# Handing over a pair's sums bank by bank in a gated linear-recurrence block

## What is computed

```python
q, v, g = jnp.split(a @ w_in, [HG_KEY_W, HG_KEY_W + HG_VAL_W], axis=-1)
z = jnp.einsum('bld,wdk->wblk', a, w_f).astype(f32)
z = jnp.clip(z, -GATE_CLIP, GATE_CLIP)
log_f = jax.nn.log_sigmoid(z) + jnp.log1p(lb * jnp.exp(-z))
k = _heads((1.0 - lb) * jax.nn.sigmoid(-z), HG_HEADS)
q = _heads(jax.nn.silu(q.astype(f32)), HG_HEADS) * (HG_DK ** -0.5)
v = _heads(v.astype(f32), HG_HEADS)
```

## Time and profile before

| what | us |
|---|---|
| median of 3 runs | 1992.04 (1991.76 to 1995.71) |
| the profiled execution | 1992.16 |
| its span, first to last instruction | 1990.4 |
| TensorE busy | 1855.9 (93%) |
| VectorE busy | 1289.5 (65%) |
| ScalarE busy | 885.1 (44%) |

### The profile page before, as it was taken

How to read it: one execution, slowest core, us unless ns; L and a number is a source line. 1 busy time by engine, 2 the same in 40 slices (tenths; PEclk the granted TensorE clock), 3 DMA queues, 4 the chain that set the end, 5 groups by cost and what they waited for, 6 DMA issues and landing times.

```text
span 1990.4 us, 32031 instructions
## 1 busy us (share of the span) xinstructions
PE 1855.9 (93%) x13348; PEld 1699.5 (85%) x13348; DVE 1289.5 (65%) x1995; ACT 885.1 (44%) x1197; POOL 0.2 (0%) x4
## 2 busy tenths in 40 slices
PE   6668999999999999999879999999999999999998
PEld 3217888889888879898779988999999999999997
DVE  5686387878797868796995556555545555444445
ACT  5555254435353525363644445333333333344444
POOL 0000000000000000000000000000000000000000
PEclk9899999999999999999999999999999999999999
DMA  7884454444444444444466545777667676555553
GB/s 270 278 279 153 161 167 127 139 143 140 130 138 129 148 142 143 135 130 135 153 202 210 180 149 152 220 214 229 213 215 219 219 218 203 173 185 180 184 183 110
DMA packets 175378, 353.20 MB, mean 177 GB/s; under 512 B 12737, under 2 KB 80642, under 8 KB 174594
## 3 DMA queue, kind: packets, MB, share of 16 engines
q1 hardware_dynamic: 175234, 351.16, 55.1%
HBM read 346.92 MB, written 4.19 MB: 176 GB/s over the span
## 4 chain that ended last, share of the span: by engine, by line
PE 75%; DVE 17%; issue 3%; ACT 2%; DMA 2%; SPq 0%; ACTq 0%; DVEq 0%
PE bank L1048 18%; PE bank L1049 17%; PE bank L1050 17%; DVE wlo L628 4%; DVE aacc L714 3%; PE score L1151 2%; PE bank L1083 2%; PE bank L1084 2%; PE bank L1085 2%; DMA raw<-in_w_ada_dram 2%; DVE work L776 1%; PE score L1048 1%; PE score L1049 1%; PE score L1050 1%; DVE work L806 1%
## 5 line engine op out<-in xcount | busy, mean ns | idle before, releaser
L628 DVE TENSOR_TENSOR wlo<-raw,whi 128x1024 fp32r<-128x1024 f32 x520 | 636.3, 1224 | 558.0 <-ACT whi L389 557.3
L389 ACT ACTIVATE whi<-raw 128x1024 fp32r<-128x1024 f32 x520 | 551.2, 1060 | 906.2 <-PE bank L1050 654.3
L1048 PE MATMUL bank<-ahi,whi 128*128 128x256 f32 (+1 forms) x2912 | 894.9, 307 | 44.9 <-DVE wlo L628 19.6
L1049 PE MATMUL bank<-alo,whi 128*128 128x256 f32 (+1 forms) x2912 | 884.8, 304 | 0.0
L1050 PE MATMUL bank<-ahi,wlo 128*128 128x256 f32 (+1 forms) x2912 | 884.2, 304 | 0.0
L1048 PEld LDWEIGHTS bank<-ahi,whi 128*128 128x128 f32 x2912 | 561.2, 193 | 76.5 <-DVE wlo L628 23.7
L1050 PEld LDWEIGHTS bank<-ahi,wlo 128*128 128x128 f32 x2912 | 561.3, 193 | 21.4
L1049 PEld LDWEIGHTS bank<-alo,whi 128*128 128x128 f32 x2912 | 561.6, 193 | 19.0
L1083 PE MATMUL bank<-whi,ahi 128*128 128x256 f32 x512 | 150.7, 294 | 17.2 <-DVE arena L732 9.9
L714 DVE SCALAR_TENSOR_TENSOR aacc<-aw,cs,aacc 128x1024 f32<-128x1024 f32 x120 | 153.4, 1278 | 4.1 <-DMA aw<-in_w_ada_dram 3.5
L1084 PE MATMUL bank<-wlo,ahi 128*128 128x256 f32 x512 | 145.8, 285 | 0.0
(11 more groups left out here) (199 smaller groups left out, 1756.4 us busy)
## 6 DMA issues: line engine op xcount, KB each, us to landing
aw<-in_w_ada_dram SPq DMA_DIRECT2D x128, 512.0 KB, 4.8
raw<-in_ffn_w_gate_dram SPq DMA_DIRECT2D x88, 512.0 KB, 3.8
raw<-in_ffn_w_up_dram SPq DMA_DIRECT2D x88, 512.0 KB, 3.7
...
raw<-in_hg_w_in_dram SPq DMA_DIRECT2D x128, 256.0 KB, 3.0
raw<-in_hg_w_f_dram SPq DMA_DIRECT2D x128, 256.0 KB, 3.1
...
```

Of the source, the lines that this page charges most:

```text
L389: act.activation(whi[:, ck % SPL, :], raw[:, ck % RAW, :], ACT.Copy).then_inc(s_hi, 1)
L628: dve.tensor_tensor(wlo[:, ck % SPL, :], raw[:, ck % RAW, :], whi[:, ck % SPL, :].bitcast(F32), ALU.subtract).then_inc(s_lo, 1)
L1048: pe.matmul(dst, w, ah, start=start, stop=False, skip_group_check=True)
L1049: pe.matmul(dst, w, al, start=False, stop=False, skip_group_check=True)
```

## The change

Three things are done, in the VQ and Z chunks alone:

- TensorE's order within a chunk. In chunk 7, both slices of bank 0 come first, then bank 1, then bank 2, and TensorE signals `s_vd` as bank 0 and bank 1 are complete. In chunk 15 the order is bank 0, 2, 1, 3, with `s_zd` after each of the first three. Chunks 0 and 8 (`r == 0`) likewise take a bank's two slices one behind the other: chunk 8 does bank 3, then 0, 1, 2, and chunk 0 does bank 0, 2, 1. The other chunks keep their order. TensorE's part of the scan stays in the middle of the chunk.
- The values are copied by ScalarE, in place of VectorE, right behind the `hi` of chunk 8 and ahead of its scan steps, each bank as it is complete.
- VectorE clips the gates right behind the `lo` of chunk 16, ahead of scan steps and `ada`, three of the banks on their own signal, and the last on `s_used`.

The core of the diff:

```diff
@@ ScalarE
+            def values(pr):
+                if pr >= 2:
+                    act.wait_ge(s_o, 2 * pr - 2)
+                for i in range(2):
+                    act.wait_ge(s_vd, 2 * pr + i + 1)
+                    act.activation(vals[pr % 2][:, 2 * i:2 * i + 2, :], bank[i][:, :].rearrange("p (t v) -> p t v", t=2),
+                                   ACT.Copy).then_inc(s_vev, 1)
...
             for ck, kind, u, r, tasks in positions():
                 if ck > C_B + KD // 2:
                     hi(ck)
+                if kind == "Z" and r == 0:
+                    values(u)
@@ VectorE
             def clip_gates(pr):
-                dve.wait_ge(s_used, C_B + 16 * (pr + 1))
...
                 for i, (d, h) in enumerate(UNITS):
+                    if i < 3:
+                        dve.wait_ge(s_zd, 3 * pr + i + 1)
+                    else:
+                        dve.wait_ge(s_used, C_B + 16 * (pr + 1))
...
-            def values(pr):
-                dve.wait_ge(s_used, C_B + 16 * pr + 8)
...
                     lo(ck)
+                p = ck % 16
+                if p == 0 and C_B + 16 <= ck <= C_G:
+                    clip_gates((ck - C_B) // 16 - 1)
...
-                if kind == "Z" and r == 0:
-                    values(u)
-                if p == 0 and C_B + 16 <= ck <= C_G:
-                    clip_gates((ck - C_B) // 16 - 1)
@@ TensorE
+            def chunk_vq(ck, r, u, between):
+
+                if r == 0:
+                    order = ((0, 0), (1, 0), (0, 2), (1, 2), (0, 1), (1, 1))
+                elif r == 7:
+                    order = ((0, 0), (1, 0), (0, 1), (1, 1), (0, 2), (1, 2))
+                else:
+                    order = ((0, 0), (0, 2), (0, 1), (1, 0), (1, 2), (1, 1))
+                for i, (a, f) in enumerate(order):
+                    if i == 3:
+                        beside(ck, between)
...
+                    last = q_bank(ck, r, a, u) if f == 2 else v_bank(ck, r, a, u, f)
+                    if r == 7 and a == 1 and f < 2:
+                        last.then_inc(s_vd, 1)
+                last.then_inc(s_used, 1)
+
+            def chunk_z(ck, r, u, between):
+                if r == 0:
+                    order = [(a, f) for f in (3, 0, 1, 2) for a in range(2)]
+                elif r == 7:
+                    order = [(a, f) for f in (0, 2, 1, 3) for a in range(2)]
+                else:
+                    order = [(a, f) for a in range(2) for f in (3, 0, 1, 2)]
+                for i, (a, f) in enumerate(order):
+                    if i == 4:
+                        beside(ck, between)
+                    last = z_bank(ck, r, a, u, f)
+                    if r == 7 and a == 1 and f < 3:
+                        last.then_inc(s_zd, 1)
+                last.then_inc(s_used, 1)
```

More of the change, by code:

```diff
@@ L209, in build @@
         s_used = sem("chunk_used")
+        s_vd = sem("v_bank_summed")
+        s_zd = sem("z_bank_summed")
         s_aw = [sem(f"aw_in{i}") for i in range(2)]
@@ L1050, in three, with v_bank @@
                 return pe.matmul(dst, wl, ah, start=False, stop=stop, skip_group_check=True)
+            def v_bank(ck, r, a, u, half):
+                s, k = ck % SPL, 2 * r + a
+                first, end = k == 0, k == KD - 1
+                if first and u:
+                    pe.wait_ge(s_zc, 4 * (u - 1) + 1 + 2 * half)
+                o = slice(512 * a, 512 * a + 256)
+                for t in (2 * half, 2 * half + 1):
+                    dst = bank[half][:, (t % 2) * T:(t % 2 + 1) * T]
+                    tk = slice(t * P, (t + 1) * P)
+                    st = first and t % 2 == 0
+                    pe.matmul(dst, ahi[:, k, tk], whi[:, s, o], start=st, stop=False, skip_group_check=True)
+                    pe.matmul(dst, ahi[:, k, tk], wlo[:, s, o], start=False, stop=False, skip_group_check=True)
+                    last = pe.matmul(dst, alo[:, k, tk], whi[:, s, o], start=False, stop=end, skip_group_check=True)
+                return last
@@ new lines, in q_bank @@
+            def q_bank(ck, r, a, u):
+                s, k = ck % SPL, 2 * r + a
+                first, end = k == 0, k == KD - 1
+                if first and u:
+                    pe.wait_ge(s_zc, 4 * (u - 1) + 2)
+                for f in range(2):
+                    o = slice(512 * a + 256 + f * P, 512 * a + 256 + (f + 1) * P)
+                    last = three(bank[2][:, f * T:(f + 1) * T], whi[:, s, o], wlo[:, s, o],
+                                 ahi[:, k, T:TT], alo[:, k, T:TT], first and f == 0, end)
+                return last
@@ new lines, in z_bank @@
+            def z_bank(ck, r, a, u, f):
+                s, k = ck % SPL, 2 * r + a
+                first, end = k == 0, k == KD - 1
+                if first and f == 3:
+                    if u:
+                        pe.wait_ge(s_zc, 4 * u)
+                        if ada_ended(ck):
+                            pe.wait_ge(s_av, ada_ended(ck))
+                if first and f < 2:
+                    pe.wait_ge(s_vev, 2 * u + f + 1)
+                if first and f == 2:
+                    pe.wait_ge(s_qev, u + 1)
+                o = slice(512 * a + f * P, 512 * a + (f + 1) * P)
+                return three(bank[f][:, :], whi[:, s, o], wlo[:, s, o], ahi[:, k, :], alo[:, k, :], first, end)
@@ new lines, in beside @@
+            def beside(ck, between):
+                for j, n in between:
+                    scan(j, n)
+                for e in ada_ends(ck):
+                    sum_modulation(e)
+            def chunk_vq(ck, r, u, between):
[8 more added lines that the diff above has]
+                        beside(ck, between)
+                    k = 2 * r + a
+                    if u == 0:
+                        pe.wait_ge(s_al, 2 * (k + 1))
+                    last = q_bank(ck, r, a, u) if f == 2 else v_bank(ck, r, a, u, f)
+                    if r == 7 and a == 1 and f < 2:
+                        last.then_inc(s_vd, 1)
+                last.then_inc(s_used, 1)
@@ L1052, in chunk @@
             def chunk(ck, kind, r, u=0, between=()):
+                if kind == "VQ":
+                    return chunk_vq(ck, r, u, between)
+                if kind == "Z":
+                    return chunk_z(ck, r, u, between)
                 s = ck % SPL
@@ L1056, in chunk @@
                     if a:
[L1057 to L1060, removed]
+                        beside(ck, between)
                     k = 2 * r + a
                     first, end = k == 0, k == KD - 1
-                    if ck < C_B + 8 and kind == "VQ":
-                        pe.wait_ge(s_al, 2 * (k + 1))
                     if kind == "FF" and u == 0:
@@ L1066, in chunk @@
                         pe.wait_ge(s_al, 2 * KD + k + 1)
[L1067 to L1107, removed]
@@ new lines, in chunk @@
+                    tk = slice(T, TT) if kind == "G" else slice(0, T)
+                    bb = 2 * (u % 2)
+                    for f in range(4):
+                        if kind == "G" and u == 0 and first and f % 2 == 0:
+                            pe.wait_ge(s_zc, 4 * (PAIRS - 1) + 1 + f)
+                        o = slice(512 * a + f * P, 512 * a + (f + 1) * P)
+                        last = three(bank[bb + f // 2][:, (f % 2) * T:(f % 2 + 1) * T], whi[:, s, o], wlo[:, s, o],
+                                     ahi[:, k, tk], alo[:, k, tk], first and f % 2 == 0, end)
```

6 lines of the change are left out of this document (removed).

## The result

| | us |
|---|---|
| before, median of 5 runs | 1993.47 (1991.76 to 1995.71) |
| after, median of 5 runs | 1983.41 (1980.55 to 1985.21) |
| after / before | 0.9947 (95%: 0.9932 to 0.9961) |
| profiled execution of after | 1985.21, span 1983.4 |

The change makes the kernel 0.53% faster, 10 us, where 1982 and 10 us were forecast. The profiled execution is the slowest of the five. It began the first pair at 156.5 us, the one of before at 153.9, and nothing that the change touches lies ahead of that; so it also entered its first chunk 8 late, at 196.48 us against 193.52. So I compare stretches, not spans. From the first chunk 8 to the last gate matmul the traces have 749.7 us before and 739.3 after: 10.4 gained. In the output-gate stage behind it some 0.5 is lost again.

The account below looks back on a forecast made before the run. TensorE, busy for 93% of the span, was taken as the bound, with its waits for the values' copy and clips to gain; 13.8 + 2.3 - 6.0 = 10.1 us gave 1982 us, range 1975 to 1989.

Parts of the forecast that it names:

- Values, chunk 8: Windows of the eight chunk 8s: 73.0 us before, 58.3 after, 59.2 with an addition for chunk 9; 13.8 us gained.
- The 0.9 for VectorE in chunk 9: Pairs 3, 5 and 6: VectorE has more work there than TensorE has in chunk 9; 3 x 0.3 us added.
- That pair 4 would lose: Chunk 8 of pair 4 becomes 7.7 us long, where it was 6.6; it loses 1.1 us.
- Clips: Chunks 16 to 18: clips at the head of VectorE's list gain 2.3 us, as VectorE bounds these chunks.
- Clock: New gaps in front of seven chunk 9s: half of them lower TensorE's clock, 3.5 x 1.7 = 6.0 us lost.
- Order on TensorE: Both slices of a bank in a row: same number of matmuls with the same weights, worth nothing.
- Values on ScalarE: Chunk 8: TensorE's whole wait on values goes, ScalarE's chain comes 1.3 us later; 13.8 us gained, 6.0 in pair 1.
- All waits go: Rival: waits and falls at values and clips all vanish, ScalarE's chain not being next; 41 us gained, 1951; chance 0.04.
- ScalarE is held twice: Rival: the norm in seven pairs is delayed 2.6 us, not 1.3; with all clock falls 1997; chance 0.06.
- VectorE absorbs it: Rival: the Z chunks' gain returns as waits for `wlo` in full VQ chunks; about 1989; chance 0.10.

Follow-up runs that it names:

- e8: The change with values on VectorE behind the `lo` of chunk 8, `hi` of chunk 9 before the queries' SiLU, no `ada` in chunks 16 to 18; 1963.88 us.
- e3: The change with the clips put back behind scan and `ada` on VectorE, keeping TensorE's order and the ScalarE copy; 1983.71 us.
- e1: The change with only TensorE's order and signals kept, values and clips back in their old places on VectorE; 1986.82 us.
- e9: The change with `hi` of chunk 9 before the queries' SiLU and values of pairs 2 to 8 on VectorE behind chunk 8's `lo`; 1962.91 us.
- e4: The change with ScalarE doing the `hi` of chunk 9 ahead of the queries' SiLU and its table loads; 1967.19 us.
- e2: The change with the values put back on VectorE behind scan and `ada`, keeping TensorE's order and the clips' new place; 1980.15 us.
- e5: The change with the values copied by VectorE, bank by bank, right behind the `lo` of chunk 8; 1976.52 us.

## Why the prediction was right

- **Values, chunk 8.** Forecast 5.7, 7.0, 7.5, 7.7, 7.5, 7.5, 7.7, 7.7; measured 6.07, 6.76, 7.41, 7.57, 7.40, 7.40, 7.58, 7.59. The sum is 57.8 where 58.3 was forecast. The 0.9 for VectorE in chunk 9 was too little: the chunk 9s are 6.3 us longer than before, of which three falls of 1.55 (under Clock, below) are 4.65, so 1.7 is left: 0.3 each in pairs 3, 5 and 6, as forecast, and 0.1 to 0.15 in each of the five others, which had been left out. Both together are 59.5, not 59.2. The chain on ScalarE was read as it ran, 0.1 too long. That pair 4 would lose came true: 6.59 to 7.57.
- **Clips.** Forecast 2.3 us, measured 2.2 over the seven windows: 1.1, 0.1, 0.95, -0.2, 0.1, 0, 0.15. VectorE is the bound there, shown by e8.
- **Clock.** Forecast 3.5 falls and 6.0 us; three falls, in the chunk 9s of pairs 4, 7 and 8. Each chunk 9 with a fall is 7.17 us, and 5.62 in e3 where the same gap brought none (last section), so 1.55 us each, 4.7 together: a fall was priced 0.15 too high, and there was half a fall less.
- **Order on TensorE: "nothing"** is the step that failed, and it failed without harm to the sum. By itself the order is worth 6.6 us (e1), since three more matmuls stand ahead of the wait and falls of the clock go with it. The working of the values used it ("six matmuls of bank 3 in front") and so had it inside the 13.8 us; what was wrong was to write it down as worthless. Had only the order been changed, this line would have missed the result.
- **Values on ScalarE** carries a sum that is right and a credit that is not. The 13.8 us were the comparison with the kernel before, in which order and copy go together. Apart, the order gives most of it, and the ScalarE copy gives 6 us in pair 1 and costs 2.8 us in the seven others, up to 7.4 with the falls of the clock that its gaps brought (e1 to e3).
- **The rivals.** "All waits go" asked that ScalarE's chain not be next; in after it was. e9 shows that the rival's 5.5 us a chunk were to be had, with the `hi` out of that chain and the values of pairs 2 to 8 back on VectorE; the `hi` alone (e4) gave 6.2 to 6.4 in most pairs. "ScalarE is held twice" didn't come: the delay was 1.2, not 2.6. "VectorE absorbs it" didn't either: the other VQ chunks of the pairs sum to 207.7 us before and 207.9 after, the other gate chunks to 314.1 and 314.5.
- **Luck in the last microsecond.** The three terms as measured give 13.5 + 2.2 - 4.7 = 11.0 us, not 10.1. The other chunks and the output-gate stage took 0.6 and 0.5 of it back, which the forecast had at nothing. And three falls is what one trace had: e3, with gaps of the same length, had two.

What stays open: by ratios e2 is 0.15% better than the full change, which the intervals can't decide. The traces begin the first pair between 152.7 and 158.0 us over the kernels, with no edit ahead of that, and this spread goes into every single execution.

## What to carry to other kernels

Before a copy goes to a less busy engine, read that engine's list up to what others wait for next: here ScalarE was busy for 45% of the span and for 7.5 of 7.6 us in the chunk where it got the copy, and the delay came out at the chunk's end in full (the `hi` of chunk 9 1.2 us later than in e5, the chunk 1.2 us longer). The cheapest cure was to take the one instruction that others wait for (`hi`) out of the end of the list, ahead of two table loads. And an order change on the engine that waits was not "nothing": count the work that stands ahead of its wait, before and after.

## What the runs showed of the chip

**The clock fell behind gaps that are alike, and not always.** Three of the three gaps of 1.93 to 1.95 us in after were followed by 1.2 GHz for a part of chunk 9. e3 has the same gap in the same place, pair 4, and no fall; its pair 7 has one. Windows of e3, chunk 8 and chunk 9 of pair 4, then chunk 9 of pair 7:

```profile
478.05:485.63 7.58, 5.66 (x26) 4.31 (x24) 2.33 (x3) 7.52 (x12) 0.00 (x0) 1.00 0.30 101
485.63:491.25 5.62, 5.62 (x25) 4.62 (x25) 5.62 (x15) 2.29 (x8) 0.00 (x0) 1.00 0.58 188
...
787.68:794.85 7.17, 7.17 (x24) 5.76 (x25) 7.17 (x17) 2.28 (x8) 0.00 (x0) 0.76 0.67 207
```

In front of a chunk 9 no gap of 1.67 us or less was followed by a fall in any trace, though one of 1.65 in a chunk 8 was, in the kernel before. Of the six gaps of 1.91 to 1.95 us in after and e3, five were. What an edit saves in a gap can so come with, or without, 1.55 us more. In e2 pair 3's chunk 8 is 8.05 us and in e1 9.58, with the same idle time in it (9.58 - 7.44 = 2.14 and 8.05 - 5.89 = 2.16): the difference is the clock (0.82 against 1.00). The Trainium skill, "TensorE: Matmul & The Clock Gate", Part 1, says that the gate's phase is its own; these pairs of like gaps agree with that, but don't show what the phase is.

**A table load cost its 1.28 us and no more.** In the timeline of after the instruction behind each load starts 0.01 us after its end (479.52 + 1.28 = 480.80, then 480.81). The price of the SiLU lies in its two loads, 2.56 us of ScalarE, over 4 times its own 0.60.
